# Two-layer mLSTM and attention trunk: copies of products go ahead of forms on ScalarE, and block forms are made piecewise, at the start of each run of crossed pairs

## What is computed

```python
def sq_relu_mlp(y, w_up, w_down):          # w_up 1024 x 4096, w_down 4096 x 1024
    u = y @ w_up
    return jnp.square(jax.nn.relu(u)) @ w_down
# in each layer: h = h + sq_relu_mlp(rmsnorm(h, norm_gains[i, 1]), mlp_w_up[i], mlp_w_down[i])
```

## Time and profile before

| | |
|---|---|
| median of 3 runs | 1260.34 us (1258.9 to 1261.13) |
| the profiled execution | 1261.75 us |
| its span, first to last instruction | 1259.9 us |
| PE, PEld busy | 94%, 91% |
| DVE, ACT, POOL busy | 79%, 60%, 9% |
| mean granted TensorE clock | 0.975 of full |

### The profile page before, as it was taken

The page is one execution under the profiler, slowest core; times in us unless marked ns, Lnnn a source line. Parts: engine busy times, 40 slices in busy tenths (PEclk is TensorE's granted clock), DMA queues, the critical chain, the costliest instruction groups (busy, mean ns, idle before and its releaser), DMA issues. The chain is left out here.

```text
span 1259.9 us, 23136 instructions
## 1 busy us (share of the span) xinstructions
PE 1185.6 (94%) x8881; PEld 1140.7 (91%) x8881; DVE 993.3 (79%) x1471; ACT 757.3 (60%) x1335; POOL 114.4 (9%) x171
## 2 busy tenths in 40 slices
PE   9999999989799799799999999999897988979998
PEld 8999999989799799799999999988787978969988
DVE  6888897887788788786568898878787887987853
ACT  6678786554465464555357878866555645645643
POOL 3311211100100100111010000001001001001000
PEclk9999999999899899899999999999998998999999
DMA  7343422522552552473132222225226435445532
GB/s 172 98 109 84 113 80 80 169 76 68 111 144 83 108 138 93 103 203 129 56 91 61 68 67 67 67 68 170 67 71 146 120 80 138 118 107 120 178 101 67
DMA packets 152375, 131.88 MB, mean 105 GB/s; under 512 B 23208, under 2 KB 143072, under 8 KB 152288
## 3 DMA queue, kind: packets, MB, share of 16 engines
q1 hardware_dynamic: 141600, 104.93, 27.8%
q0 software_dynamic: 10560, 25.66, 10.6%
q10 hardware_dynamic: 128, 0.09, 0.0%
HBM read 111.43 MB, written 19.24 MB: 104 GB/s over the span
## 5 line engine op out<-in xcount | busy, mean ns | idle before, releaser
L2314 PE MATMUL ps<-yl,hi 128*128 128x264 f32 (+1 forms) x408 | 120.1, 294 | 49.3 <-ACT pu L761 49.3
L1648 DVE TENSOR_TENSOR lo<-lof,hi 128x1024 fp32r<-128x1024 f32 x92 | 112.3, 1223 | 67.7 <-ACT hi L761 67.5
L2031 PE MATMUL ps<-yh,wh 128*128 128x264 f32 (+1 forms) x704 | 160.5, 302 | 0.0
L2031 PE MATMUL ps<-yh,wl 128*128 128x264 f32 (+1 forms) x704 | 155.3, 295 | 0.0
L2031 PE MATMUL ps<-yl,wh 128*128 128x264 f32 (+1 forms) x704 | 155.3, 295 | 0.0
L761 ACT ACTIVATE hi<-lof 128x1024 fp32r<-128x1024 f32 x92 | 96.1, 1053 | 69.7 <-DVE lof L1641 69.7
L2314 PE MATMUL ps<-th,hi 128*128 128x264 f32 (+1 forms) x448 | 128.2, 286 | 10.4 <-ACT pu L761 10.2
L2314 PE MATMUL ps<-tl,hi 128*128 128x264 f32 (+1 forms) x448 | 127.6, 285 | 0.0
L2314 PE MATMUL ps<-th,lo 128*128 128x264 f32 (+1 forms) x448 | 127.5, 285 | 0.0
L2314 PEld LDWEIGHTS ps<-yl,hi 128*128 128x128 f32 x408 | 80.9, 198 | 50.5 <-DVE lo L1648 50.4
L761 ACT ACTIVATE hi<-raw 128x1024 fp32r<-128x1024 f32 (+1 forms) x128 | 111.9, 896 | 22.9 <-DMA raw<-in_mlp_w_up_dram 21.4
(11 more groups left out here) (328 smaller groups left out, 3466.8 us busy)
## 6 DMA issues: line engine op xcount, KB each, us to landing
raw<-in_mlp_w_up_dram SPq DMA_DIRECT2D x32, 1024.0 KB, 6.8
raw<-in_mlp_w_down_dram SPq DMA_DIRECT2D x32, 1024.0 KB, 4.9
raw<-in_diff_w_in_dram SPq DMA_DIRECT2D x24, 512.0 KB, 3.8
raw<-in_mlstm_w_in_dram SPq DMA_DIRECT2D x16, 512.0 KB, 4.6
h_sum<-abuf POOLq DMA_DIRECT2D x24, 264.0 KB, 4.5
h_sum<-abuf POOLq DMA_DIRECT2D x24, 256.0 KB, 4.9
h_sum<-h POOLq DMA_DIRECT2D x16, 264.0 KB, 2.4
h<-h_sum POOLq DMA_DIRECT2D x2, 2112.0 KB, 12.6
```

Of the source, the lines that this page charges most:

```text
L1648: V.tensor_tensor(lo[1 - i % 2][:, rows, :], lof[1 - i % 2][:, rows, :], hi[1 - i % 2][:, rows, :].bitcast(F32), ALU.subtract).then_inc(m_ ...
L2031: last = mm(ps[:, bank + s, 0:w_], w[:, slot, kb, :], m[:, kb, t0:t0 + w_], start=(kb == 0 and n == 0), stop=(kb == CB - 1 and n == 2))
L2314: last = mm(ps[:, bank, 0:w], x[1 - i % 2][:, at, :], y, start=(kb == 0 and n == 0 and name in ("A11", "S1", "A12")), stop=(kb == 3 and n ...
```

## The change

On ACT, where a run begins, P1 and P5 (with the squaring of the pair before, or the high part of block form S3, between them) and U2 now stand ahead of the high part of the next pair's forms S14; `block_hi(i, "A22")` comes between U2 and the forms. In the second matrix U2 also goes ahead of the forms in the pairs that do not begin a run. On DVE the fourth block form (A22) is made after the low part of S1's; the low part of block form S3 goes ahead of the low part of the next forms S14. Waits on `b_made` ask for as many block forms as are needed, not for all four. No instruction is added or taken away; the programs of PE, SP and POOL keep their order.

```diff
@@ ACT: block_hi
-                    act.wait_ge(b_made, 4 * ((GROUPS - 1) * layer + i // 8 + 1))
+                    act.wait_ge(b_made, 4 * ((GROUPS - 1) * layer + i // 8) + BLOCK_MADE[name])
@@ ACT: the loop over the pairs
+                    if begins:
+                        snap(i, "P1")
+                        if is_up(i):
+                            squares(i - 1, 1)
+                        else:
+                            block_hi(i, "S3")
+                        snap(i, "P5")
+                    if crossed(i) and (begins or not is_up(i)):
+                        snap(i, "U2")
+                    if begins and not is_up(i):
+                        block_hi(i, "A22")
                     if crossed(i + 1):
                         form_hi(i + 1, "S14")
-                    if begins and not is_up(i):
-                        block_hi(i, "S3")
-                        block_hi(i, "A22")
-                    if begins:
-                        snap(i, "P1")
-                        snap(i, "P5")
-                    if crossed(i):
+                    if crossed(i) and is_up(i) and not begins:
                         snap(i, "U2")
                     if crossed(i + 1):
                         form_hi(i + 1, "S23")
@@ DVE: block_lo and the loop over the pairs
-                    dve.wait_ge(b_made, 4 * ((GROUPS - 1) * layer + i // 8 + 1))
+                    dve.wait_ge(b_made, 4 * ((GROUPS - 1) * layer + i // 8) + (3 if name in ("S1", "S3") else 4))
...
-                        block_forms(i)
+                        block_forms(i, ("S3", "S1", "S2"))
+                    if begins and not is_up(i):
+                        block_lo(i, "S3")
                     if crossed(i + 1):
                         form_lo(i + 1, "S14")
                     if begins and not is_up(i):
-                        block_lo(i, "S3")
                         block_lo(i, "A22")
...
                     if sent_down(i) and i % 8 == DOWN_FROM - 1:
                         block_lo(i, "S1")
+                        if DOWN_FROM == 5:
+                            block_forms(i, ("A22",))
                         block_lo(i, "S2")
```

More of the change, by code:

```diff
@@ L132 @@
 BLOCK_ORDER = ("S1", "S2", "S3", "A22")
+BLOCK_MADE = {"S3": 1, "S1": 2, "S2": 3, "A22": 4}
 BANK = {"A12": 0, "S1": 1, "S4": 1, "A11": 2, "S2": 2, "S3": 2, "A22": 2}
@@ L1124, in mlp @@
                         form_hi(i + 1, "S23")
-                    if i > 0 and not in_tail(layer, i - 1) and not sent_down(i - 1) and not (sent_down(i) and i % 8 == 4):
+                    if i > 0 and not in_tail(layer, i - 1) and not sent_down(i - 1) and not (sent_down(i) and i % 8 == 4) and not begins:
                         finish(i - 1, 1)
@@ L1680, in act_lo, with block_forms @@
                                     ALU.subtract).then_inc(a_ready, 1)
-                def block_forms(i):
+                def block_forms(i, names):
                     made = 4 * ((GROUPS - 1) * layer + i // 8)
                     b11, b12, b21, b22 = (blocks_f[:, :, n, 0:w] for n in range(4))
[L1686 to L1694, removed]
+                    for name in names:
+                        if name == "S3":
+                            dve.wait_ge(sqa_done, block_of(i - 1, 1) + 1)
+                            dve.wait_ge(a_ready, block_of(i - 1, 1) + 1)
+                        else:
+                            dve.wait_ge(b_made, made + BLOCK_MADE[name] - 1)
+                        o, x, y, op = {"S3": (b22, b22, b12, ALU.subtract), "S1": (b12, b12, b11, ALU.subtract),
+                                       "S2": (b11, b22, b11, ALU.add), "A22": (b21, b21, b11, ALU.subtract)}[name]
+                        V.tensor_tensor(o, x, y, op).then_inc(b_made, 1)
                 def block_lo(i, name):
                     n = BLOCK_FORM[name]
-                    dve.wait_ge(b_made, 4 * ((GROUPS - 1) * layer + i // 8 + 1))
+                    dve.wait_ge(b_made, 4 * ((GROUPS - 1) * layer + i // 8) + (3 if name in ("S1", "S3") else 4))
                     dve.wait_ge(b_hi, form_count(layer, i, name))
@@ L1764, in mlp @@
                         act_lo(i - 1, 0)
+                    if sent_down(i) and i % 8 == 4 and DOWN_FROM > 5:
+                        block_forms(i, ("A22",))
                     if sent_down(i) and i % 8 == DOWN_FROM - 1:
                         block_lo(i, "S1")
+                        if DOWN_FROM == 5:
+                            block_forms(i, ("A22",))
                         block_lo(i, "S2")
```

## The result

The changed kernel takes **1211.64 us** in the median of 4 runs (1211.05 to 1213.43), the kernel before 1259.72 beside it on the same chip: a ratio of 0.962, with a 95% interval of 0.9603 to 0.9636. The gain of 48.1 us stands against a forecast of 51, the time against 1209.4.

A forecast was written before the change was run, and what follows sets the result against it. PE, 94% busy, sets the time; its waits, mostly for ACT's `pu`, can be won. 3 x 7.4 + 3 x 6.3 + 4.4 + 5.5 = 51 us off 1261.75 gives 1210.8, or 1209.4 against the median; range 1204 to 1222.

The forecast's parts named there:

- The wait of S2 was for P1 in ACT's order: Pair 5: PE idled 8.22 us before S2 for ACT's copy P1, queued behind pair 6's forms; the change ends that wait.
- The rival that S2 waited for something else: S2 hangs on the low part of pair 6's forms, only pair 2 gains: 1250 us, chance 0.04.
- The new wait before S2, 1.6 us: Pair 5: S2 next waits for DVE's low part of weights S23, starting at 317.9; 1.6 us instead of 8.2.
- The new wait before S3, 2.6 us: Pair 5: S3 waits for DVE's low part of block form S3, done at 323.4; 2.6 us.
- Second matrix in layer 0, 7.4 us each: Pairs 5, 13, 21: A22 of pair 5 starts at 327.9 against 335.26, a gain of 7.4 us per start.
- Second matrix in layer 1, 6.3 each: Three starts, same chain with slightly shorter block-form steps: A22 at 954.3 against 960.64, a gain of 6.3 us each.
- Pair 2, 4.4 and 5.5: First matrix: S2 starts at once, then C22 is late; gains of 4.4 us in layer 0, 5.5 in layer 1.
- U2 moved, nothing: Pairs 6, 7 and their like: U2 ahead delays the forms' high part at most 1.2 us, 12 times; no cost taken.
- Pair 7's load has 1 us of cover: Load lands at 326.1, P1 of pair 6 is made by 328.3, S2 of pair 6 wants it at 329.3.
- The rival of the clock: The clock falls at the second new wait, before S3, six times, adding 10 us: 1219 us, chance 0.19.
- The signs of being wrong: `pu` before S2 of pair 6, clock 0.5 after S3's wait, ACT's `raw` wait over 1 us, hole before S1 of pairs 7, 8.

The follow-up runs named there:

- the third experiment: The changed kernel with U2 again behind the high part of the next forms S14 in pairs that do not begin a run: 1212.03 us.

## Why the prediction was right, and where it was off

- *The wait of S2 was for P1 in ACT's order.* Right. `pu` fell from 59.6 to 1.6 us, and with ACT's order undone S2 starts at 325.63 again, 0.14 us after P1. The rival that S2 waited for something else would have given 1250.
- *The new wait before S2, 1.6 us.* Measured 1.29 in layer 0 and 1.69 in layer 1. S2 starts at 313.40, which is 317.73 with the 4.33 us of pair 2 added; 317.9 was worked out. Counting DVE's steps from its first block form was enough for this.
- *The new wait before S3, 2.6 us.* Measured 2.26 and 2.32. S3 starts at 318.84, or 323.17 with the shift, against 323.4.
- *Second matrix in layer 0, 7.4 us each.* This is **the step that was mis-sized**: 6.16, 6.43 and 6.73, 2.9 us less in all. The prediction took no fall of the clock at the second new wait; it fell at all three of these, and filling that wait gave some 1.25 us each. 324.77 + 4.33 = 329.1 for A22 of pair 5, against 327.9: 21.2 us after the first block form, not 20.0. The reason given for taking nothing (PE was not idle for longer together) is not what decides: with the first wait filled the clock fell as well.
- *Second matrix in layer 1, 6.3 each.* 6.42, 6.54 and 6.59; here the clock stayed at 2.4 GHz in the profiled execution.
- *Pair 2, 4.4 and 5.5.* 4.33 and 5.16; A22 at 287.08 against 287.1, with the 0.7 us wait for C22 measured as 0.62. The chain was right, the hit to the last digit is luck: the steps as listed add up to 5.9 us, which gives 286.9. In layer 1 the sum took 5.7, and A22 came 0.3 us later than that (889.41 + 23.8 = 913.2 against 912.9).
- *U2 moved, nothing.* Right, by the third experiment.
- *Pair 7's load has 1 us of cover.* Right that it is near, too small by a little: ACT waited 1.21 us for the load, P1 of pair 6 ran at 323.51, and PE reached S2 of pair 6 only at 326.24 (324.77 + 1.47), without a wait.
- *The rival of the clock* had the right mechanism for three of the six starts, and the price of 1.65 us that was kept for it is near the 1.5 us of PE's time and the 1.25 per start that were measured. Nothing in the prediction says why three and not six: with U2 behind the forms it was four, with the first wait filled five. That the time came within 2.2 us of the forecast owes something to this.
- *The signs of being wrong.* Two of them came, a granted clock of 0.52 after S3's wait and an ACT wait of 1.21 us for `raw`; the first cost some 3.8 us, the second nothing.

Against a sum of 51, the eight starts gave 48.4: 2.9 less in layer 0, 0.7 more in layer 1, 0.4 less at the two pairs 2. That is the miss of 2.2 us in the time. The profiled executions differ by 50.3, because the one before also holds the late weight load at pair 26, 1.8 us that the change did not win. The profiled execution before stood 1.4 us over its median, that of the changed kernel (1211.47) stands at its median (1211.64), which fits a load that is late in some executions only. Only one execution before was traced, so this cause of the offset is not shown.

The Trainium skill ("TensorE: Matmul & The Clock Gate", section "Why this matters for your kernels") advises against idle gaps above a length that none of the new waits reaches. By that rule the sum would have held. These runs do not bear it out: 2.26 us in the change, and 1.77 us with S3's low part early, were followed by the half clock.

**What stays open.** All fourteen profiles together hold these waits of PE from the first MLP on: of 1.24 to 1.76 us, 71, none of them followed by the half clock; of 1.77 to 1.90 us, 19, of which 8 were; of 2.24 to 2.32 us, 24, of which 14 were (10 of 12 in layer 0, 4 of 12 in layer 1); of 3.38 us and more, 28, all of them. 1.77 us fell where 1.90 did not, 2.24 fell at one start and not at the next two of the same kernel. Between 1.77 and 2.32 us the length of the wait alone does not decide; what does was not found.

## What to carry to other kernels

Where an engine works in written order, look for the smallest instruction that another engine waits for and ask what stands ahead of it that itself waits: here the copy was one of 0.4 us behind three large steps. ACT's new order, of which it is the main piece, gave 27 of the 48 us alone, and without it the rest of the change gave 2. Then work out at once what is late next, by adding up the steps of the engine that feeds it; when that engine has no hole, a reordering moves the last wait rather than ending it, and what is left to win is the length of the chain. Where a wait of some 2 us cannot be removed, matmuls of no use in it did not delay S3 here (318.93 against 318.84) and gave 5.5 us in the median by keeping the clock.

## What the runs showed of the hardware

- **The clock fell after shorter waits than expected**, 2.26 us and, in other kernels, 1.77 to 1.88 us (8 of 19 waits of 1.77 to 1.90), and stayed at the half level for 14 matmuls at each of the three starts of the changed kernel. With fillers in the last wait of a start (1.5 to 1.6 us left, or 0.9 and less) it did not fall in any start of three profiles.
- **GpSimd holds VectorE up.** A difference of 128x1056 float32 elements took POOL 3.31 us, and the DVE instruction begun after it 3.53 instead of 1.25: it ended at 312.91, 1.1 us after POOL's, at 311.79, which is about its own time. The DVE instruction that was under way when POOL's began, from 308.25, kept its 1.22 us; whether POOL's 3.31 us hold a wait for it is not shown, as POOL was never run alone at this size. The Trainium skill ("SBUF — State Buffer", section "SBUF: two separate sides") says that the port pair the two share goes to one of them for a whole instruction, for a DVE instruction with two inputs in SBUF too. The trace agrees; that the port is the cause was not tested by itself.
